# The modulation product shared between TensorE and VectorE, and the last square of the layers' norms summed by TensorE

## The reference, cut to what matters

```python
# first block: modulation; c and c_ctx are vectors of 1024, w_ada is 1024 x 6144
mx = (silu(c) @ w_ada + b_ada)[:, None, :]
mc = silu(c_ctx) @ w_ada + b_ada
xsh1, xsc1, xg1, xsh2, xsc2, xg2 = split(mx, 6)
csh1, csc1, cg1, csh2, csc2, cg2 = split(mc, 6)
px = split_in((x * (1 + xsc1) + xsh1) @ w_in)        # 512 tokens
pc = split_in((ctx * (1 + csc1) + csh1) @ w_in)      # 256 context tokens
...
# the block has one layer, so of mc only csh1 and csc1 are used; mx is used whole

# second block, two layers: five norms of this kind, over the 1024 features of a token
def _rmsnorm(x, g):
    return x * rsqrt(mean(x * x, -1) + 1e-6) * g
```

## Time and profile before

| what | value |
| --- | --- |
| timed executions | 4633.06 to 4638.51 us, median 4634.1 us |
| the profiled execution's own time | 4641.54 us |
| its span, first to last instruction | 4639.8 us |
| granted TensorE clock, mean | 0.971 |
| TensorE (PE) busy | 4322.8 us, 93% |
| VectorE (DVE) busy | 2629.2 us, 57% |
| ScalarE (ACT) busy | 1809.5 us, 39% |
| bytes read from HBM | 553.99 MB |
| first phase | from 0 to 104.85 us |
| the five norms | the totals are multiplied at 2836.8, 3360.3, 3730.8, 4254.0 and 4624.8 us |

### The profile page before, as it was taken

How to read it: one execution, slowest core, us unless ns; L and a number is a source line. 1 busy time by engine, 2 the same in 40 slices (tenths; PEclk the granted TensorE clock), 3 DMA queues, 4 the chain that set the end, 5 groups by cost and what they waited for, 6 DMA issues and landing times. The chain is left out here.

```text
span 4639.8 us, 54117 instructions
## 1 busy us (share of the span) xinstructions
PE 4322.8 (93%) x20775; PEld 3482.1 (75%) x20775; DVE 2629.2 (57%) x4611; ACT 1809.5 (39%) x2555; POOL 502.3 (11%) x308
## 2 busy tenths in 40 slices
PE   8988888978998988999999997999999999999998
PEld 6767666646874566999999995777788877787887
DVE  0777767784445987777777774344433343534332
ACT  1655655443322133333333334454332234633222
POOL 0000000000002611444444430000000000000000
PEclk9999999989999988999999998999999999999999
DMA  7111111102222246988888872212323322122332
GB/s 271 62 41 42 37 37 46 41 14 95 91 86 77 70 158 243 319 298 297 302 303 299 299 249 73 64 57 75 98 89 95 96 91 64 48 91 89 96 96 82
DMA packets 203059, 589.31 MB, mean 127 GB/s; under 512 B 18112, under 2 KB 73664, under 8 KB 201280
## 3 DMA queue, kind: packets, MB, share of 16 engines
q1 hardware_dynamic: 164944, 444.78, 28.7%
q0 software_dynamic: 36864, 134.23, 8.2%
q10 hardware_dynamic: 1008, 7.03, 0.4%
HBM read 553.99 MB, written 31.98 MB: 126 GB/s over the span
## 5 line engine op out<-in xcount | busy, mean ns | idle before, releaser
L386 DVE TENSOR_TENSOR tile_rest<-tile_raw,tile_up 128x1024 fp32r<-128x1024 f32 (+2 forms) x288 | 338.7, 1181 | 761.1 <-ACT tile_up L377 760.9
L394 PE MATMUL layer_psum<-hn_up,tile_up 128*128 128x512 f32 x1344 | 534.1, 397 | 21.2 <-DVE hn_rest L481 21.2
L395 PE MATMUL layer_psum<-hn_up,tile_rest 128*128 128x512 f32 x1344 | 527.4, 392 | 0.0
L396 PE MATMUL layer_psum<-hn_rest,tile_up 128*128 128x512 f32 x1344 | 527.1, 392 | 0.0
L377 ACT ACTIVATE tile_up<-tile_raw 128x1024 fp32r<-128x1024 f32 (+2 forms) x288 | 291.5, 1018 | 382.0 <-PE layer_psum L396 368.5
L394 PEld LDWEIGHTS layer_psum<-hn_up,tile_up 128*128 128x128 f32 x1344 | 255.1, 190 | 82.3 <-issue 30.0
L2308 PE MATMUL ex_psum<-ex_v_up,ex_prod_up 128*128 128x512 f32 x768 | 299.4, 390 | 2.3 <-DVE ex_prod_rest L2416 2.3
L2310 PE MATMUL ex_psum<-ex_v_rest,ex_prod_up 128*128 128x512 f32 x768 | 300.6, 391 | 0.0
L2312 PE MATMUL ex_psum<-ex_v_up,ex_prod_rest 128*128 128x512 f32 x768 | 300.5, 391 | 0.0
L395 PEld LDWEIGHTS layer_psum<-hn_up,tile_rest 128*128 128x128 f32 x1344 | 255.3, 190 | 54.4 <-issue 1.9
L396 PEld LDWEIGHTS layer_psum<-hn_rest,tile_up 128*128 128x128 f32 x1344 | 254.9, 190 | 53.9
(11 more groups left out here) (464 smaller groups left out, 10117.3 us busy)
## 6 DMA issues: line engine op xcount, KB each, us to landing
tT<-in_peer_v SPq DMA_DIRECT2D x128, 512.0 KB
ex_u<-in_peer_u SPq DMA_DIRECT2D x104, 512.0 KB
tile_raw<-in_w_gu SPq DMA_DIRECT2D x88, 512.0 KB
xT<-in_w_head SPq DMA_DIRECT2D x56, 512.0 KB
mod_w<-in_w_ada SPq DMA_DIRECT2D x48, 512.0 KB, 4.7
mg_w_raw<-in_w_merge SPq DMA_DIRECT2D x48, 512.0 KB, 3.5
expert_table<-et_rows SPq DMA_DIRECT2D x6, 4096.0 KB, 11.5
ex_rows<-expert_table SPq DMA_DIRECT2D x64, 384.0 KB, 6.7
```

The lines of the kernel that those rows point to most:

```text
L386: self.nc.vector.tensor_tensor(out=self.rest[:, n % self.SLOTS, 0:blocks, :], in0=self.raw[n % self.RAWS][:, 0:blocks, :], in1=self.up[:, ...
L394: self.nc.tensor.matmul(dst, w_up, up, start=first, stop=False)
L395: self.nc.tensor.matmul(dst, w_rest, up, start=False, stop=False)
L396: return self.nc.tensor.matmul(dst, w_up, rest, start=False, stop=last)
```

## The change

`FIRST_PARTS = 2`: TensorE computes the first two of the six parts as before (shift and scale of the mixers, for both vectors). The other four parts, needed for `c` alone, come to VectorE. Their weights are laid out the other way round, as 32 tiles of `[128, 1024]` (512 KB each) in which a partition holds all 1024 weights of one output; `sil_rows` holds silu of `c` in every partition. One instruction multiplies a tile by it and sums along the row, which gives 128 outputs as a column. The tiles go through six slots that lie in activation tensors not yet in use. SP issues the two kinds in turn, 16 pairs, and then the other 16 row tiles. In the norms VectorE no longer adds the eighth square; TensorE multiplies the total of seven and the eighth square one after the other into the same bank.

```diff
+FIRST_PARTS = 2
@@ class RunningNorm
     def gather(self, nc, dve, k):
-        if k == 0:
+        if k == 0 or k == DB - 1:
             return
@@
     def pe(self, nc, pe):
-        pe.wait_ge(self.gathered, START + DB - 1)
-        nc.tensor.matmul(self.bank, self.mean, self.total, start=True, stop=True).then_inc(self.spread, 1)
+        pe.wait_ge(self.gathered, START + DB - 2)
+        nc.tensor.matmul(self.bank, self.mean, self.total, start=True, stop=False)
+        pe.wait_ge(self.squared, START + DB)
+        nc.tensor.matmul(self.bank, self.mean, self.sq[(DB - 1) % 2], start=False, stop=True).then_inc(self.spread, 1)
@@ phase_modulation
-        w = ph.stream(8, [(6, 8, list(range(8)))])
+        w = ph.stream(8, [(FIRST_PARTS, 8, list(range(8)))])
-        rows = ph.sb("rows", [2, 6 * D])
+        rows = ph.sb("rows", [2, FIRST_PARTS * D])
+        sil_rows = mem.xT[:, 4:6, :].rearrange("p b t -> p (b t)")
+        slots = [tiles[:, b:b + 2, :].rearrange("p b t -> p (b t)")
+                 for tiles, b in ((mem.hgT, 0), (mem.hgT, 2), (mem.hgT, 4), (mem.hgT, 6), (mem.convT, 4), (mem.convT, 6))]
+        MOD_TILES = (6 - FIRST_PARTS) * DB
+        landed, summed = [ph.sem(f"landed{n}") for n in range(len(slots))], ph.sem("summed")
+        rows_loaded, rows_ready = ph.sem("rows_loaded"), ph.sem("rows_ready")
@@ sync
-            with sp.Fori(0, 6) as i:
-                for k in range(8):
-                    load_tile(sp, w, 0, k, i, io["w_ada"][i, k])
+            def load_rows(m):
+                if m >= len(slots):
+                    sp.wait_ge(summed, START + m - len(slots) + 1)
+                sp.dma_start(slots[m % len(slots)], io["w_ada_rows"][m]).then_inc(landed[m % len(slots)], 16)
+
+            for n in range(FIRST_PARTS * DB):
+                load_tile(sp, w, 0, n % DB, n // DB, io["w_ada"][n // DB, n % DB])
+                load_rows(n)
+            for m in range(FIRST_PARTS * DB, MOD_TILES):
+                load_rows(m)
@@ scalar
             act.dma_start(mem.par[:], io["params"]).then_inc(loaded, 16)
+            act.dma_start(sil_rows, io["cond_rows"]).then_inc(rows_loaded, 16)
...
             nc.scalar.activation(sil[:], cond[:], ACT.Silu).then_inc(sil_ready, 1)
-            with act.Fori(0, 6) as i:
+            act.wait_ge(rows_loaded, START + 16)
+            nc.scalar.activation(sil_rows, sil_rows, ACT.Silu).then_inc(rows_ready, 1)
+            with act.Fori(0, FIRST_PARTS) as i:
@@ tensor
-            with pe.Fori(0, 6) as i:
+            with pe.Fori(0, FIRST_PARTS) as i:
...
-            pe.wait_ge(row_out, START + CREDIT + 12)
+            pe.wait_ge(row_out, START + CREDIT + 2 * FIRST_PARTS)
-            for m in range(48):
+            for m in range(DB * FIRST_PARTS):
@@ vector
+            dve.wait_ge(rows_ready, START + 1)
+            for m in range(MOD_TILES):
+                row, at = slots[m % len(slots)], FIRST_PARTS * DB + m
+                dve.wait_ge(landed[m % len(slots)], START + 16 * (m // len(slots)) + 16)
+                nc.vector.tensor_tensor_reduce(out=row, in0=row, in1=sil_rows, scale=1.0, scalar=0.0, op0=ALU.mult,
+                                               op1=ALU.add, accum_out=mem.mod[:, at, 0:1]).then_inc(summed, 1)
+            rest = mem.mod[:, FIRST_PARTS * DB:6 * DB, 0]
+            seq = Order(dve, order)
+            seq.body(0, 4)
+            dve.wait_ge(summed, START + MOD_TILES)
+            seq(nc.vector.tensor_tensor(out=rest, in0=rest, in1=mem.p("b_ada")[:, FIRST_PARTS * DB:6 * DB], op=ALU.add))
+            seq(nc.vector.tensor_scalar_add(mem.mod[:, 4 * DB:5 * DB, 0], mem.mod[:, 4 * DB:5 * DB, 0], 1.0))
             dve.wait_ge(x_loaded, START + 64)
             nc.vector.tensor_copy(mem.masks[:], masks[:]).then_inc(copied, 1)
             dve.wait_ge(copied, START + 1)
-            seq = Order(dve, order)
-            seq.body(0, 2)
             dve.wait_ge(turned, START + 1)
-            bias = mem.par[:, PARAM_AT["b_ada"]].unsqueeze(2).to_broadcast([P, 48, 2])
-            seq(nc.vector.tensor_tensor(out=mem.mod[:], in0=B[2][:, 0:96].rearrange("p (m c) -> p m c", c=2),
-                                        in1=bias, op=ALU.add))
-            parts = mem.mod[:].rearrange("p (h q b) c -> p h q (b c)", h=2, q=3)
-            seq(nc.vector.tensor_scalar_add(parts[:, :, 1, :], parts[:, :, 1, :], 1.0))
+            n = DB * FIRST_PARTS
+            bias = mem.p("b_ada")[:, 0:n].unsqueeze(2).to_broadcast([P, n, 2])
+            seq(nc.vector.tensor_tensor(out=mem.mod[:, 0:n, :],
+                                        in0=B[2][:, 0:2 * n].rearrange("p (m c) -> p m c", c=2), in1=bias, op=ALU.add))
+            seq(nc.vector.tensor_scalar_add(mem.mod[:, DB:2 * DB, :], mem.mod[:, DB:2 * DB, :], 1.0))
@@ layouts
-    out["w_ada"] = tiles(a["w_ada"][0]).reshape(6, 8, P, DB, P)
+    out["w_ada"] = tiles(a["w_ada"][0]).reshape(6, 8, P, DB, P)[:FIRST_PARTS]
+    out["w_ada_rows"] = a["w_ada"][0][:, FIRST_PARTS * D:].T.reshape(-1, P, D)
+    out["cond_rows"] = np.tile(a["c"][0].reshape(1, D), (P, 1))
```

## The result

The changed kernel takes 4610.8 us (median of 5, 4609.1 to 4616.4) against 4634.1 before. The ratio over all runs is 0.9947 with a 95% interval of 0.9936 to 0.9959, 19.0 to 29.7 us less (the two medians alone give 0.9950). The forecast was 4610.0 us, faster. Its profiled execution took 4610.79 us.

What follows compares the result with a forecast made beforehand. TensorE was taken to bound the first phase from 40 us on, and transfers after the change. Gains of 22.9 (phase) and 1.5 us (final norm) less 0.3 (semaphores) took 4634.1 to 4610.0 us, range about 4606 to 4615.5.

Steps and rivals of the forecast that it cites:

- TensorE bounds the phase from 40 us on, and the transfers have room: First phase before the change: from 40 us TensorE sets the pace, transfers run at 299 GB/s against 408 earlier.
- The last byte at 77.9 us: First phase: the 15.47 MB left at 40 us take 37.9 us at 408 GB/s, so transfers end then.
- Its landing: First phase: semaphore of the last byte's transfer, taken as 1.0 us, between 0 and 2.5.
- One sum, then bias, masks and bias: First phase's tail on VectorE after the last landing: 2.99 us, ending the phase at 81.9 us.
- TensorE's part is hidden: First phase: TensorE's 16 tiles, done at 63 us even at half clock, and transposes finish before the last row tiles come.
- The ring does not bind: First phase: six row-tile slots with a 6.0 us round trip allow one tile each 1.0 us, enough for the transfers.
- Four norms worth 0: Four of five norms: no gain, since Ln waits for ScalarE's own queue and the first product runs during the last block.
- The sum: Whole kernel: 22.9 us from the first phase plus 1.5 from norms minus 0.3 for semaphores, 24.1 us less.
- (a): First phase: last 16 row tiles come slower than 408 GB/s; 4617.5 us at 299 GB/s; chance 0.12.
- (b): First phase, second half: VectorE's sums at half speed, 2.44 us, set the pace; 4626.1 us; chance 0.05 with similar losses.
- (c): Whole first phase: VectorE's sums collide with transfers and set the pace; 4654.0 us at 3.6 us each; chance 0.03.
- (d): Next phase's start: idle TensorE stays at half clock 2 us longer, costing 1 us; 4611.0 us; within the forecast's 0.80.

## Why the prediction was right, point by point

The mechanism was right for the first phase, which carries nearly all of the gain, and for the final norm. Two terms were off by about a microsecond each, the last landing and the first norm.

- **TensorE bounds the phase from 40 us on, and the transfers have room.** Right. With a third of the products left, the rate holds at 409 GB/s, and taking bytes away ends the phase 8.2 us sooner.
- **The last byte at 77.9 us.** Right for the bulk: the rate was 418 GB/s from 77.0 to 77.5 us and 279 from there to 78.0, and then fell to 49 and below.
- **Its landing.** This was the step that was mis-sized. I took 1.0 us. A thin stream went on after 78.0, 49 GB/s in the first half us and 8 in the fourth, and the last sum started at 80.17 us (80.03 with three parts, where VectorE stood waiting for it). That is 2.1 to 2.3 us after 77.9, within the bounds of 0 to 2.5. It is 1.1 to 1.3 us more than I took and explains the 1.1 us by which the phase ended later than 81.9; the shorter tail (next point) gave 0.2 back.
- **One sum, then bias, masks and bias.** 2.82 us from the start of the last sum, against 2.99. VectorE's own pace is 1.145 us, the lower of my bounds, not the 1.30 that I took; it decided nothing, as the transfers were slower. But one sign was wrong. I had written that VectorE without idle time after 57 us would mean that it paces the phase. It showed none from 60 us on, and the transfers paced it all the same: its start to start time fell from 1.28 to 1.145 us when less had to be loaded.
- **Semaphores.** The gap between the phases grew from 2.82 to 2.93 us, 0.1 us and not 0.3.
- **TensorE's part is hidden.** Right: its transposes ended at 62.3 us, 18 us before the last landing. Where that cover is gone, with three parts, the phase ends 1.1 us later.
- **The ring does not bind.** Right, with 5.8 us of round trip measured.
- **The final norm, 1.5 us.** Right: 1.55, and the table load is what ends last there now.
- **Four norms worth 0.** Wrong for one. The step that failed is that the first product would run while the last block is added and squared. At the first norm the squares come 0.8 us apart with no products before them, so there is little to run beside, and both products stand on the path at half clock (the first starts 0.2 us behind the end of the last square). That costs 0.8 us, which was in no term of the sum, and Ln waits for TensorE at a norm, which I had said it would not. I had read one `mx_` norm and carried it over. For the third norm I also took one execution for the rule: its 0 is 0.5 to 0.6 us when the clock has fallen, as in two of the three profiles with the old norms.
- **The sum.** Measured locally 21.8 + 0.75 = 22.5 us, foretold 24.1, and 23.3 by the medians. The terms were 1.6 us too high in all. That the forecast of 4610.0 came within 0.8 us of the median is partly luck, for the interval of the measured gain is over 10 us wide.

The rivals: (a) did not hold, the rate stayed at 409 to 410 GB/s until 75 us. The Trainium skill's figure of about 358 GB/s per core for loads from HBM (DMA: Bandwidth & Descriptors, section Specifications) was exceeded here for 50 us, by a kernel that ran on one core alone. (b) did not hold either: the 32 sums took 1225 ns on average, and doubling them showed what it would have looked like. The Trainium skill states halved throughput for one instruction shape, `S2S2D2_STT` (Vector Engine (DVE) Microarchitecture Reference, section Points that are easy to get wrong). It does not say whether `tensor_tensor_reduce` has this shape; if it has, these sums contradict the rule. (c) fell with the same run: no collision at full rate. (d) cost nothing: TensorE idled 29.6 us, and its products took 0.79 and then 0.63 us as before. In this profile they got short after 3.6 us in place of 5.3, but in two others of the new modulation after 5.3 again, so that is no gain of the change.

## What to carry to other kernels

When one engine paces a stage that only streams weights, ask what the transfers could do at most, and read it from the stretch where they run ahead. Giving work to an idle engine then brings the difference between the two paces; here it brought no more when the shares were changed from two parts to three. And a wait taken off an engine is worth something only where that engine ends last: read each instance of a helper by itself, because the same few lines gained 1.55 us at one norm and lost 0.8 at another, gained nothing at two, and at the third norm gained nothing or half a microsecond, as the clock stood. In the three norms in the middle an unrelated cut in ScalarE's queue had to move before the full gain showed.

## What was not expected of the hardware

- A stage can be paced by transfers and show an engine as nearly always busy (19.35 of 20 us) with no wait in the timeline. The start to start time (1.28 against its own 1.145 us) tells it.
- The last tile of a full queue landed about 2 us after the bulk of the traffic had ended at 78 us, in six profiles alike (the last sum starts at 80.0 to 80.2 us).
- The same product of two instructions, after the same 2.17 us of idling, took 1.12 us in one execution (granted clock 1.00) and 1.95 and 2.08 us in two others (0.52 and 0.50).
